# Low parts of the first expert block's down matrix on GpSimd, and the next rows' low part one place earlier on VectorE

## The reference

```python
def run_block(args):
    xblk, e = args                      # 128 rows, one expert of 32
    h = jax.nn.silu(xblk @ w_gate[e]) * (xblk @ w_up[e])    # 1024 -> 512
    return h @ w_down[e]                                     # 512 -> 1024
yb = lax.map(run_block, (xb, block_e)).reshape(P, D)
y = jax.ops.segment_sum(yb * slot_w[:, None].astype(yb.dtype), slot_tok, num_segments=N)
```

## Time and profile before

| what | value |
|---|---|
| runs shown | 1749.19, 1751.72, 1754.18 us |
| span of the profiled execution, first to last instruction | 1746.6 us |
| PE busy in the span | 1699.8 us (97%) |
| DVE busy | 1048.1 us (60%) |
| ACT busy | 864.4 us (49%) |
| POOL busy | 251.0 us (14%) |
| chain that ended last: share of PE | 86% |
| mean granted TensorE clock | 0.992 |

### The profile page before, as it was taken

The page is one execution under the profiler, slowest core; times in us unless marked ns, Lnnn a source line. Parts: engine busy times, 40 slices in busy tenths (PEclk is TensorE's granted clock), DMA queues, the critical chain, the costliest instruction groups (busy, mean ns, idle before and its releaser), DMA issues.

```text
span 1746.6 us, 27562 instructions
## 1 busy us (share of the span) xinstructions
PE 1699.8 (97%) x8254; PEld 1377.5 (79%) x8254; DVE 1048.1 (60%) x1287; ACT 864.4 (49%) x1137; POOL 251.0 (14%) x353
## 2 busy tenths in 40 slices
PE   8999999999999999989999999999999999999985
PEld 7888888888888776778888877778888888888862
DVE  3114655641111255754356864699999999999946
ACT  3232332322232566323232311588888888888844
POOL 0012222220000000100000005031111111111100
PEclk9999999999999999999999999999999999999997
DMA  7342323331232536774234425699999999999748
GB/s 257 115 130 104 114 99 129 129 130 61 97 119 104 174 115 218 254 263 151 96 106 164 150 85 156 239 425 414 397 394 398 387 390 387 396 382 391 302 149 321
DMA packets 119932, 388.29 MB, mean 222 GB/s; under 512 B 23986, under 2 KB 35634, under 8 KB 95300
## 3 DMA queue, kind: packets, MB, share of 16 engines
q1 hardware_dynamic: 93620, 315.30, 48.6%
q0 software_dynamic: 26256, 72.25, 11.5%
HBM read 335.24 MB, written 69.07 MB: 231 GB/s over the span
## 4 chain that ended last, share of the span: by engine, by line
PE 86%; DVE 5%; DMA 4%; issue 2%; ACT 1%; SPq 1%; DVEq 0%; POOL 0%; ACTq 0%; POOLq 0%
PE ps L931 47%; PE ps L1281 19%; PE ps L1305 10%; PE ps L1230 2%; PE ps L1221 2%; DMA a_n<-arena 1%; PE ps L982 1%; PE ps L1053 1%; PE ps L1080 1%; PE ps L1131 1%; PE ps L1069 1%; PE ps L1291 1%; DMA arena<-in_expert_w_gate 1%; PE ps L1145 1%; DMA arena<-b_t 1%
## 5 line engine op out<-in xcount | busy, mean ns | idle before, releaser
L1369 ACT ACTIVATE act_h<-arena 128x1024 fp32r (+2 forms) x292 | 292.9, 1014 | 76.2 <-PE ps L1305 37.4
L2184 DVE TENSOR_TENSOR act_l<-arena,act_h 128x1024 fp32r<-128x1024 f32 x256 | 306.2, 1223 | 21.1 <-ACT act_h L1369 13.4
L931 PE MATMUL ps<-act_h,wgt_h 128*128 128x512 f32 x728 | 287.4, 395 | 6.6 <-DVE wgt_l L1771 5.7
L1369 ACT ACTIVATE arena<-ps 128x512 f32<-128x512 f32 (+4 forms) x259 | 142.1, 576 | 294.1 <-PE ps L931 239.7
L931 PE MATMUL ps<-act_h,wgt_l 128*128 128x512 f32 x728 | 284.3, 390 | 0.0
L931 PE MATMUL ps<-act_l,wgt_h 128*128 128x512 f32 x728 | 284.3, 390 | 0.0
L1369 ACT ACTIVATE wgt_h<-arena 128x1024 fp32r (+2 forms) x216 | 222.1, 1050 | 88.0 <-PE ps L931 70.3
L931 PE MATMUL ps<-wgt_h,act_h 128*128 128x512 f32 (+1 forms) x640 | 248.6, 388 | 0.1
L931 PE MATMUL ps<-wgt_h,act_l 128*128 128x512 f32 (+1 forms) x640 | 242.8, 379 | 0.0
L931 PE MATMUL ps<-wgt_l,act_h 128*128 128x512 f32 (+1 forms) x640 | 242.4, 379 | 0.0
L1369 ACT ACTIVATE arena<-arena 128x512 f32<-128x512 f32 (+4 forms) x124 | 65.1, 539 | 331.2 <-DVE arena L1816 108.4
(11 more groups left out here) (202 smaller groups left out, 2472.2 us busy)
## 6 DMA issues: line engine op xcount, KB each, us to landing
arena<-in_expert_w_gate SPq DMA_DIRECT2D x64, 1024.0 KB
arena<-in_expert_w_up SPq DMA_DIRECT2D x64, 1024.0 KB
arena<-in_expert_w_down SPq DMA_DIRECT2D x64, 1024.0 KB
arena<-in_w_in SPq DMA_DIRECT2D x12, 2048.0 KB, 9.2
z_t<-arena POOLq DMA_DIRECT2D x56, 256.0 KB, 2.3
arena<-z_t SPq DMA_DIRECT2D x40, 256.0 KB, 3.3
arena<-y_n SPq DMA_DIRECT2D x16, 512.0 KB, 8.5
kv_n<-arena POOLq DMA_DIRECT2D x24, 256.0 KB, 2.3
```

The source lines that it names most:

```text
L931: ins = pe.matmul(out, left(x, k), right(y, k), start=k == 0 and (x, y) == (0, 0), stop=k == KC - 1 and x == 1)
L1369: return act.activation(out, in_, f, **kw)
L2184: dve.tensor_tensor(dst[:, w * c:w * (c + 1), :], arrived(src, m, b, slice(w * c, w * (c + 1))), f(high[:, w * c:w * (c + 1), :]), ALU.sub ...
```

## The change

```diff
@@ gpsimd @@
-            for b in range(1, 3):
-                pool.wait_ge(xt_done, 2 * b)
-                gather(b, b)
+            pool.wait_ge(xt_done, 2)
+            gather(1, 1)
+            pool.wait_ge(xt_done, 4)
+            gather(2, 2)
+            for c in range(WC):
+                pool.wait_ge(m_hi[2], c + 1)
+                pool.tensor_tensor(d_l[:, c:c + 1, :], arrived(ring_down, 2, 0, slice(c, c + 1)),
+                                   f(d_h[:, c:c + 1, :]), ALU.subtract).then_inc(m_lo[2], 1)
             with pool.Fori(3, n_blocks) as b:
@@ vector, block_step @@
                 if not first and not last:
+                    x_low(b + 1)
                     low_expert(1, b + 1, u_l, u_h, ring_up, range(WC - 1, WC))
-                    x_low(b + 1)
...
-                low_expert(2, b, d_l, d_h, ring_down)
+                if not first:
+                    dve.wait_ge(m_lo[2], b * WC)
+                    dve.sem_inc(t_dve, 1)
+                    low_expert(2, b, d_l, d_h, ring_down)
                 hid_low(b)
```

## The result

The changed kernel takes 1755.64 us (median of 9 runs, 1753.1 to 1757.68) against 1750.05 us for the kernel before (9 runs, 1749.19 to 1754.18): a ratio of **1.0031, 95% interval 1.0023 to 1.0040**, or 5.4 us more (0.31% of 1750.05). The interval leaves out 1, so it is slower, and it sits on the 0.3% that the prediction took as the bound of "no change". The span went from 1746.6 to 1752.5 us, the mean granted clock from 0.992 to 0.991. The lines of the changed kernel are five higher in this stage: L2184 is now L2189, L1281 is L1286, L1291 is L1296, L2112 is L2117, L2227 is L2232; POOL's subtractions are L903. In the experiments they shift again by a few lines.

The account below looks back on a forecast made before the run. PE was taken as the bound, idling only where the loop fills. New waits of 4.3 and 2.3 us less the old 2.3 added 4.2 to 1751.7: 1755.9 us; range 1749.4 to 1762, the forecast's own 1753.5 to 1758.

Parts of the forecast that it names:

- the forecast's 4.2: Start of gate(2) on PE: 4.2 us later, from new waits of 4.3 and 2.3 us less the old 2.3.
- the clock at 0: PE between the two predicted waits in block 0's down product: slower clock costs 0, upper end 2 us.
- the price: POOL's subtraction of 128x1024: 2.45 us each, unhindered.
- the moved `x_low`: On DVE, `x_low` ahead of one chunk: rows 1.14 us earlier, chunk 1.14 us later, free in the loop.
- the ceiling: PE's wait for `x_low` before gate(2): the most the change could win, 2.3 us.
- SP's second half of up(3): This load would wait for POOL's fourth subtraction, until 1155.75, at a cost of 0; uncovered, a microsecond or two.
- the third step of the sum: DVE runs seven subtractions without a gap to 1149.65 while POOL waits; `hidden(1)` starts then, the old gate(2) wait goes.
- the fourth and fifth: POOL's last two subtractions end at 1152.1 and 1155.75; PE idles 4.3 and 2.3 us in block 0's down product.
- step 1: POOL's first subtraction starts when DVE's string ends, 1136.8 to 1139.25, beside DVE's `hid_low(0)`.
- POOL keeps the port: POOL's four subtractions run back to back, delaying DVE's `hidden(1)` and gate(2): +3.5 us, 1755.2 us plus clock; chance 0.20.
- Gather too late: POOL's copy for gather 3 misses its moment, PE waits for block 3's rows: 4 to 8 us more, about 1762; chance 0.20.

Follow-up runs that it names:

- experiment 2: The kernel before with only `x_low` moved ahead of the last chunk of up, all subtractions left on DVE: 1748.27 us, ratio 0.9994.
- experiment 6: The kernel before, on DVE only `hidden(1)` put ahead of up(2) and `x_low(2)` behind up(2)'s first chunk: 1747.19 us, ratio 0.9985.
- experiment 1: The changed kernel with `x_low` back in its old place, so only the four subtractions move to POOL: 1754.92 us, ratio 1.0036.
- experiment 3: The changed kernel with DVE making chunks 0 and 1 of down(0), POOL chunks 2 and 3 after them: 1749.89 us, ratio 1.0003.
- experiment 8: Experiment 7 with ACT's high parts of the rows ahead of up's, and `x_low` right behind `hidden` on DVE, early blocks only: 1749.72 us, ratio 0.9996.
- experiment 5: The changed kernel with 14 more matmuls into an unused PSUM bank while PE waits for `hidden(1)`: 1751.38 us, ratio 1.0015.
- experiment 4: The kernel before with four subtractions, results unread, added on POOL behind its last scatter: 1749.01 us, one run.
- experiment 7: Experiment 6 with 4 more matmuls in each of PE's two waits of step 0: 1747.50 us, ratio 0.9985.

## Why the prediction was right in size and wrong in mechanism

**Right: the size and the side, the size by luck.** The trace shows 4.32 us up to 1400 us against +4.2, but the parts are others: the forecast's 4.2 were waits alone with the clock at 0, and measured were 2.61 us of waits and 1.72 us of clock (its upper end was 2). The time, 1755.64 us, is 0.3 us from the forecast, by luck again: its base, 1751.72, came down to 1750.05 with more runs, while the loss was 5.4 us. The result is at the edge of 0.3%, where the prediction put it.

**Right: the price, the moved `x_low` and the ceiling.** POOL's subtraction takes 2.30 us (2.45 was taken). `x_low` ahead of one chunk gave its 1.13 us at gate(2), and left a step of the loop at 17.76 us; what it did to POOL's copies (experiment 2) was not foreseen. The wait that could be won at all is 2.37 us in experiment 6, for 2.3. SP's second half of up(3) waited for POOL (the two halves went out in 5.78 us from 1143.39 instead of 2.72), and nobody waited for the load, as forecast.

**Wrong: the third step of the sum, and the fourth and fifth with it.** The step that failed is the third: "DVE now runs 4 + 3 subtractions without a gap ... POOL waits all that time." It was read from the 4.33 us of the earlier trace rows, a copy that sat out a whole string. POOL's subtractions sat out one instruction of DVE each; the first already went ahead of the last chunk of up(1), where step 1 let it wait for the end of the string. The 4.33 us are as long as nearly four subtractions of DVE, more than a lock for one instruction explains, though the prediction found the two to agree. With that, everything behind it changes place: POOL was through at 1148.5, not 1155.75; PE met no wait inside the down product (predicted: 4.3 and 2.3 us); `hidden(1)` was late by 3.75 us instead of on time; and PE waited before the hidden transposes (3.58 us) and gate(2) (0.50 us).

**The nearest rival was the right one in place, not in its reason.** "POOL keeps the port" put the wait at `hidden(1)` and gate(2), for +3.5 us; it was 2.61. It thought POOL's four would run back to back because they stand in one queue. What was against it in the prediction, that DVE is already waiting when each ends, is just what happened: DVE got every second turn. The price is nearly the same, as in either order DVE waits for nearly every POOL instruction in full. Experiments 1 and 3 show that the loss belongs to these instructions and grows with their number (3.75 us at `hidden(1)` for four, 1.81 for two, which also stand later).

**"Gather too late" did not come, but was no idle worry.** In the changed kernel the copy for gather 3 took 1.18 us right behind the fourth subtraction. In experiments 2 and 8, where POOL subtracts nothing, copies and gathers were held 5.57 to 9.80 us, and PE waited for the rows.

**The clock was put at nothing.** The forecast took 0 because two waits inside the down product would have hidden the slow stretch. With the idle in another place, 3.58 and 0.50 us just before gate(2), it was 1.72 us, and experiment 5 gave it back. In experiment 4 the unchanged code lost 1.64 us in the same place, after 1.40 and 2.11 us.

**Not foreseen: 1.0 to 1.2 us at the end.** In the changed kernel and its repetition, the stretch from PE's last wait in the last down product to the end is that much longer. In experiments 1 and 5 it lasts 58.6 and 58.85 us, in experiments 2, 3, 4 and 6 57.2 to 57.5; but it is also 59.2 and 58.7 us in experiments 7 and 8, in which POOL subtracts nothing. The whole stretch therefore doesn't tell. Two places in it do: POOL's scatter next to the last, here before and after, and PE's wait for a load of `z_n` behind it.

```profile
1687.82 0.98 POOL L894 DMA_INDIRECT y_n<-arena  x1 [12.80 <-ACT arena L1369]
```

```profile
1692.93 2.02 POOL L894 DMA_INDIRECT y_n<-arena  x1 [13.17 <-issue]
```

In the four traces with all four subtractions on POOL (the changed kernel twice, experiments 1 and 5) the scatter starts 1.24 us after ACT's output instead of 0.87 or 0.88 and lasts 2.01 or 2.02 us, and PE waits 2.57 to 2.86 us. In the seven others the scatter lasts 0.97 or 0.98 us, and PE waits 1.69 to 2.02. So about 0.9 us of waiting go with the four subtractions, though they ended some 540 us earlier. Why the scatter is late, and whether it makes the load late, no experiment settles.

## What to carry to other kernels

Before work goes from one engine to another, price what the second takes away from the first while it runs: here a 1.14 us subtraction with two SBUF inputs, given to POOL, held DVE up by some 2.2 us, so that relief on paper was a delay of 0.9 us per chunk. Where one wait is to go, look first at what stands ahead of the late result in its own engine's order: 2.37 us at gate(2) were won by moving two short operations on DVE, and the ratio of 0.9985 bears out a gain. Follow the small instructions of a shared engine too: a copy of 128 numbers and a gather that missed their moment were held 8.98 and 9.80 us, and PE waited 3.15 us for the rows. And before a difference of one or two microseconds is read from single traces, take a second trace of the same code.

## What the runs showed of the hardware

**Turns of one instruction.** With subtractions of two SBUF inputs on both engines, DVE's began 3.35 us apart instead of 1.14 and POOL's 3.36 instead of 2.30, each within 0.1 us of the sum of both; DVE's `hid_low(0)`, with one input from PSUM, kept its 0.68 us beside POOL. The Trainium skill (SBUF — State Buffer, section "Who interferes with whom") says that the shared ports are locked for a whole instruction and that whoever issues first has them. The lengths agree with the lock; that the turn then goes to the other engine, one for one, is what the trace adds.

**But not for every POOL instruction.** POOL's copies and indirect DMAs read one number per partition. In the changed kernel the copy at 1148.45 got in after one instruction of DVE (1.18 us), and in experiment 3 one in the middle of a string took 0.61 us; others waited for the end of a string, 4.33 us, 8.98 and 9.80 us (experiment 8). What decides between the two isn't settled: no experiment was made on it.

**What an idle of PE costs afterwards.** After waits of 3.58 and 0.50 us just ahead of gate(2), the granted clock was 0.50 up to 1160.2, and 1.72 us were lost; after 2.01 us in the same place in the kernel before it was 1.00, and with the gap filled, after 0.51 and 0.88 us, the matmuls ran at the old pace (experiment 5). So a delay of 2.61 us became 4.32. The length of the waits alone does not tell what follows: in step 0 the clock fell behind waits of 0.99 and 1.08 us in the trace of the kernel before, and stayed at 1.00 behind 0.99 and 1.10 us in that of experiment 4.
